# Root mean squares of four norms by token on partitions, and six modulation chunks summed off TensorE

## The reference

```python
def rms_norm(x, gain=None):
    y = x * lax.rsqrt(jnp.mean(x * x, axis=-1, keepdims=True) + 1e-6)
    return y if gain is None else y * gain

cond = jax.nn.silu(c)
for layer in range(2):
    mod = cond @ ada_w[layer] + ada_b[layer]            # (1024) @ (1024 x 6144)
    sh_m, sc_m, g_m, sh_f, sc_f, g_f = jnp.split(mod, 6, axis=-1)
    h = rms_norm(x) * (1 + sc_m) + sh_m
    mix = dsa_mixer(h, ...) if layer == 0 else gated_deltanet_mixer(h, ...)
    x = x + g_m * mix
    h = rms_norm(x) * (1 + sc_f) + sh_f
    x = x + g_f * peer_ffn(h, ...)
return rms_norm(x, final_norm)
```

## Time and profile before

| | |
|---|---|
| time, median of 3 runs (lowest, highest) | 3556.41 us (3554.92, 3565.26) |
| the profiled execution's own time | 3563.29 us |
| its span, first to last instruction | 3561.3 us |
| mean granted TensorE clock | 0.991 |
| busy share: PE, DVE, ACT, POOL | 97%, 73%, 50%, 32% |
| attention (with norm0 and modulations), about | 0 to 340 us |
| norm1, norm2, norm3, norm4, about | 340 to 360, 1642 to 1663, 2254 to 2276, 3541 to 3561 us |

### The profile page before, as it was taken

How to read it: one execution, slowest core, us unless ns; L and a number is a source line. 1 busy time by engine, 2 the same in 40 slices (tenths; PEclk the granted TensorE clock), 3 DMA queues, 4 the chain that set the end, 5 groups by cost and what they waited for, 6 DMA issues and landing times.

```text
span 3561.3 us, 62918 instructions
## 1 busy us (share of the span) xinstructions
PE 3445.7 (97%) x20018; PEld 3155.0 (89%) x20018; DVE 2604.0 (73%) x4767; ACT 1777.1 (50%) x3224; POOL 1144.1 (32%) x866
## 2 busy tenths in 40 slices
PE   7999999999999999998999999899999999999998
PEld 4556899999999999996777697699999999999997
DVE  2755767579996888886888543576669996888887
ACT  3364345567773333335775233345557875333333
POOL 2102342534441222223664002343444442222222
PEclk9999999999999999999999999999999999999998
DMA  7564345789999999993556652235698999999995
GB/s 243 178 190 154 99 150 175 270 313 352 374 377 373 341 344 337 338 340 103 162 168 187 176 150 76 81 120 171 196 348 300 378 375 371 367 349 348 343 350 198
DMA packets 519872, 914.11 MB, mean 257 GB/s; under 512 B 70352, under 2 KB 359248, under 8 KB 511312
## 3 DMA queue, kind: packets, MB, share of 16 engines
q1 hardware_dynamic: 446032, 644.23, 52.9%
q0 software_dynamic: 73728, 268.47, 21.2%
HBM read 782.54 MB, written 130.02 MB: 256 GB/s over the span
## 4 chain that ended last, share of the span: by engine, by line
PE 81%; DVE 6%; ACT 5%; issue 3%; DMA 3%; SPq 1%; POOL 1%; DVEq 0%; ACTq 0%; POOLq 0%
PE bank L783 10%; PE bank L785 10%; PE bank L784 10%; PE bank L855 10%; PE bank L856 10%; PE bank L857 10%; PE bank L831 4%; PE bank L1010 2%; DVE oh L2592 2%; PE bank L479 2%; DVE rows L2563 1%; PE bank L1019 1%; DMA w_ring<-b_w_in 1%; PE bank L572 1%; PE bank L794 1%
## 5 line engine op out<-in xcount | busy, mean ns | idle before, releaser
L783 PE MATMUL bank<-hx,hl 128*128 128x384 f32 (+1 forms) x2304 | 798.6, 347 | 0.7 <-POOL hl L1579 0.7
L784 PE MATMUL bank<-hx,hl 128*128 128x384 f32 (+1 forms) x2304 | 786.2, 341 | 0.0
L785 PE MATMUL bank<-hx,hl 128*128 128x384 f32 (+1 forms) x2304 | 786.1, 341 | 0.0
L855 PE MATMUL bank<-W,hl 128*128 128x384 f32 x2016 | 679.8, 337 | 7.4 <-DVE W L2630 7.4
L856 PE MATMUL bank<-W,hl 128*128 128x384 f32 x2016 | 679.5, 337 | 0.0
L857 PE MATMUL bank<-W,hl 128*128 128x384 f32 x2016 | 679.5, 337 | 0.0
L1602 POOL DMA_INDIRECT rows<-p_v,erow x256 | 262.4, 1025 | 858.4 <-DVE xtok L2637 836.4
L1602 POOL DMA_INDIRECT rows<-p_u,erow x256 | 358.9, 1402 | 406.3 <-DVE rows L2563 368.0
L1910 ACT ACTIVATE hl<-hT 128x1024 fp32r<-128x1024 f32 x272 | 287.6, 1057 | 362.5 <-PE bank L857 317.4
L1910 ACT ACTIVATE hl<-w_ring 128x1024 fp32r<-128x1024 f32 x272 | 287.4, 1057 | 344.6 <-PE bank L857 311.7
L783 PEld LDWEIGHTS bank<-hx,hl 128*128 128x128 f32 x2304 | 434.6, 189 | 10.9 <-POOL hl L1579 0.9
(11 more groups left out here) (372 smaller groups left out, 5507.0 us busy)
## 6 DMA issues: line engine op xcount, KB each, us to landing
w_ring<-p_u_t SPq DMA_DIRECT2D x128, 512.0 KB
hT<-p_u_t SPq DMA_DIRECT2D x128, 512.0 KB
w_ring<-p_v SPq DMA_DIRECT2D x128, 512.0 KB
hT<-p_v SPq DMA_DIRECT2D x128, 512.0 KB
act_scratch<-hT SPq DMA_DIRECT2D x256, 192.0 KB
g_scratch<-gst SPq DMA_DIRECT2D x48, 1024.0 KB
gg<-g_scratch SPq DMA_DIRECT2D x64, 768.0 KB
ua<-act_scratch SPq DMA_DIRECT2D x256, 192.0 KB
```

The costliest lines, as they stand in the source:

```text
L783: nc.tensor.matmul(bank[s][:, c:], hi, hx[:, 0, k, c:], start=(k == 0), stop=False)
L784: nc.tensor.matmul(bank[s][:, c:], hi, hx[:, 1, k, c:], start=False, stop=False)
L785: mm = nc.tensor.matmul(bank[s][:, c:], lo, hx[:, 0, k, c:], start=False, stop=(k == KD - 1))
L855: nc.tensor.matmul(bank[j][:, P:], hi, W[:, s, 0, :], start=first, stop=False)
```

## The change

It does these things:

1. Chunks 4 to 9 of the modulations leave TensorE's row product. Chunks 4 to 7 are multiplied by the condition and summed over k on VectorE (`ada_product`, 8 instructions a chunk, in front of the scoring). Chunks 8 and 9 are multiplied in place by ScalarE (`ada_scaled`, at m = 3 and 4) and added up on GpSimd in three instructions (`ada_sums`). TensorE keeps the column products of all (`summed_columns`), at other places, and into bank 4. Chunks 10 and 11 keep their row products, behind tiles m = 6 and 7.
2. The low parts of weight tiles 2 to 7 move from GpSimd to VectorE (`in_low` in the VectorE part), between the products of item 1.
3. `INDEXED`: the last two pairs of the indexer move from tile m = 2 to m = 3, and the keys' tiles come one tile later with that.
4. The 16 rounds over tt = 1 move into the scoring of tt = 2 and 3: one "8 largest" and one strike-out for each of the 16 scores. The loop behind is over tt = 2 and 3 alone.
5. The bias of chunks 4 to 11 is added at head step 2, no longer in front of `maxima(0)`. The `+ 1` of the scales is made from the bank in one instruction.
6. Norms 1 to 4: the sums come out with tokens on partitions, as 4 columns of bank 2, by 8 products with one column of ones; root and inverse are on 128 x 4 elements; 4 products of the inverse, spread over 128 weight columns, with the identity spread it to 128 x 512 in bank 2, which VectorE then reads as its second operand instead of `rstd`. VectorE frees bank 2 behind the last of the eight multiplications.
7. The queue of transfers: chunk 6 is loaded before tile 6, chunks 7 to 9 behind tiles 7 to 9, chunks 10 and 11 behind tile 14. A chunk's slot is free when its predecessor is summed.

```diff
@@ constants
-           [(3, 0), (3, 1), (3, 2), (3, 3)]]
+           [(3, 0), (3, 1)], [(3, 2), (3, 3)]]
+ADA_FIRST, ADA_LAST = 4, 12
+ADA_BY_DVE = 8
+ADA_SCALED_AT = {8: 3, 9: 4}
+ADA_ROWS_AT = {10: 6, 11: 7}
+ADA_COLUMNS_AT = {4: -1, 5: -1, 6: 0, 7: 0, 8: 6, 9: 7}
+LOW_BY_POOL = 8
@@ TensorE, norm_added
                 take(2)
-                pe.wait_ge(sem("squares_added"), (KD - 2) * times)
-                nc.tensor.matmul(bank[2][:, :], ones[:, :], hT[:, 0, :], start=True, stop=False)
-                pe.wait_ge(sem("squares"), t.turn("squares", KD) + KD)
-                nc.tensor.matmul(bank[2][:, :], ones[:, :], hT[:, KD - 1, :], start=False, stop=True
-                                 ).then_inc(psum_full[2], 1)
+                squares = t.turn("squares", KD) + KD
+                order = (0, KD - 1) if times % 2 else (KD - 1, 0)
+                for k in order:
+                    if k == 0:
+                        pe.wait_ge(sem("squares_added"), (KD - 2) * times)
+                    else:
+                        pe.wait_ge(sem("squares"), squares)
+                    for tt in range(TT):
+                        mm = nc.tensor.matmul(bank[2][:, tt:tt + 1], hT[:, k, tt * P:(tt + 1) * P], ones[:, 0:1],
+                                              start=(k == order[0] and tt == 0), stop=(k == order[1] and tt == TT - 1))
+                mm.then_inc(psum_full[2], 1)
+
+                take(2)
+                pe.wait_ge(sem("columns_ready"), 1 + times)
+                for tt in range(TT):
+                    mm = nc.tensor.matmul(bank[2][:, tt * P:(tt + 1) * P], rstd[:, tt:tt + 1].to_broadcast([P, P]), ident[:, :],
+                                          start=True, stop=True)
+                mm.then_inc(psum_full[2], 1)
@@ TensorE, attention
-                take(3)
-                for m in range(KD):
-                    in_tile(7 + m, m % 2, between=(lambda k, m=m: indexed(m, k)) if m < len(INDEXED) else None)
-                    ada_rows(4 + m)
-                    if m > 0:
-                        ada_columns(3 + m)
+                take(4)
+                for m in range(-1, KD):
+                    if m >= 0:
+                        in_tile(7 + m, m % 2, between=(lambda k, m=m: indexed(m, k)) if m < len(INDEXED) else None)
+                    for n in ADA_ROWS_AT:
+                        if ADA_ROWS_AT[n] == m:
+                            ada_rows(n)
+                    for n in ADA_COLUMNS_AT:
+                        if ADA_COLUMNS_AT[n] == m:
+                            summed_columns(n).then_inc(sem("ada_turned"), 1)
...
-                ada_columns(11).then_inc(psum_full[3], 1)
+                summed_columns(10)
+                summed_columns(11).then_inc(psum_full[4], 1)
@@ SyncE
                 for m in range(4):
                     load_in(3 + m, C_QI + m * P)
+                    if m == 2:
+                        load_ada(6)
...
-                for m in range(2):
+                for m in range(KD):
                     load_in(7 + m, m * P)
-                for m in range(KD):
-                    if m + 2 < KD:
-                        load_in(9 + m, (m + 2) * P)
-                    if 6 + m < 12:
-                        load_ada(6 + m)
+                    if m < 3:
+                        load_ada(7 + m)
+                for n in range(10, ADA_LAST):
+                    load_ada(n)
@@ GpSimd
-            for i in range(2, 15):
+            def ada_sums(n):
+
+                part = ada_slot(n)
+                pool.wait_ge(sem("ada_scaled"), KD * (n - ADA_BY_DVE + 1))
+                pool.wait_ge(sem("ada_turned"), n - ADA_FIRST - 1)
+                for step, width in enumerate((4, 2, 1)):
+                    to = part[:, 0:width, :] if width > 1 else ada_sum(n).unsqueeze(1)
+                    if step > 0:
+                        pool.wait_ge(sem("ada_summed"), ada_summed(n - 1) + step)
+                    nc.gpsimd.tensor_tensor(to, part[:, 0:width, :], part[:, width:2 * width, :], ALU.add
+                                            ).then_inc(sem("ada_summed"), 1)
+
+            for i in range(LOW_BY_POOL, 13):
                 in_low(i)
+            ada_sums(8)
+            in_low(13)
+            ada_sums(9)
+            in_low(14)
@@ ScalarE, norm
-                nc.scalar.activation(rstd[:, :], bank[2][:, :], ACT.Sqrt, scale=1.0 / D, bias=eps[:, 0:1]
+                n = T if stage == "norm0" else TT
+                nc.scalar.activation(rstd[:, 0:n], bank[2][:, 0:n], ACT.Sqrt, scale=1.0 / D, bias=eps[:, 0:1]
                                      ).then_inc(psum_free[2], 1)
@@ VectorE
-                ins.then_inc(sem("mods_ready"), 1)
...
+                step(nc.vector.tensor_tensor(flat[:, first:last], bank[b][:, first:last], added[:, first:last], ALU.add))
                 for c in scales:
-                    ins = nc.vector.tensor_scalar(flat[:, c:c + KD], flat[:, c:c + KD], 1.0, None, ALU.add)
+                    ins = nc.vector.scalar_tensor_tensor(flat[:, c:c + KD], bank[b][:, c:c + KD], 1.0, added[:, c:c + KD],
+                                                         ALU.add, ALU.add)
...
-                step(nc.vector.reciprocal(rstd[:, :], rstd[:, :]))
+                if nth == 0:
+                    step(nc.vector.reciprocal(rstd[:, :], rstd[:, :]))
+                else:
+                    nc.vector.reciprocal(rstd[:, 0:TT], rstd[:, 0:TT]).then_inc(sem("columns_ready"), 1)
+                    full(2)
+                inverse = rstd[:, :] if nth == 0 else bank[2][:, :]
...
+                if nth > 0:
+                    dve.wait_ge(sem("hn_ready"), KD * (nth + 1))
+                    dve.sem_inc(psum_free[2], 1)
...
+                def ada_product(n, first, last):
+
+                    to = ada_sum(n)
+                    for k in range(first, last):
+                        if k == 0:
+                            dve.wait_ge(sem(f"ada_loaded{n % 2}"), 16 * (n // 2))
+                            ins = nc.vector.tensor_scalar(to, ada_slot(n)[:, k, :], cond[:, k, 0:1], None, ALU.mult)
+                        else:
+                            dve.wait_ge(sem("ada_summed"), KD * (n - ADA_FIRST) + k)
+                            ins = nc.vector.scalar_tensor_tensor(to, ada_slot(n)[:, k, :], cond[:, k, 0:1], to, ALU.mult, ALU.add)
+                        ins.then_inc(sem("ada_summed"), 1)
```

More of the change, by code:

```diff
@@ L228, in hybrid_trunk @@
         probT = sb("probT", [P, 2, 2, TT, T], where=part)
+        mx = sb("mx", [P, 8], where=part)
+        nmx = sb("nmx", [P, 8], where=part)
+        rowsum = sb("rowsum", [P, 8], where=part)
+        rinv = sb("rinv", [P, 8], where=part)
         stage_ = ExitStack()
@@ L521, in ada_columns, with summed_columns @@
                 return mm
+            def summed_columns(n):
+                if n in ADA_ROWS_AT:
+                    pe.wait_ge(psum_free[ada_bank(n)], marks[f"ada{n}"])
+                    part = ada_part[:, n % 2, :]
+                else:
+                    pe.wait_ge(sem("ada_summed"), ada_summed(n))
+                    part = ada_sum(n)
+                for c in range(4):
+                    mm = nc.tensor.matmul(bank[4][:, 4 * n + c:4 * n + c + 1], part[:, c * P:(c + 1) * P],
+                                          ones[:, 0:1], start=True, stop=True)
+                return mm
@@ L2319, in attention, with largest, taken, masked @@
                 ins.then_inc(sem("ckv_ready"), 1)
+                ada_product(5, KD // 2, KD)
+                in_low(5)
+                ada_product(6, 0, KD)
+                in_low(6)
+                ada_product(7, 0, KD // 2)
+                in_low(7)
+                ada_product(7, KD // 2, KD)
+                def largest(tt):
+                    return nc.vector.max(top8[:, tt, :], score[:, tt, 0:(tt + 1) * P])
+                def taken(tt):
+                    return nc.vector.match_replace(score[:, tt, 0:(tt + 1) * P], top8[:, tt, :],
+                                                   score[:, tt, 0:(tt + 1) * P], TAKEN)
+                def masked(tt):
+                    return nc.vector.memset(score[0:CHUNK, tt, tt * P + CHUNK:(tt + 1) * P], NEG)
                 for n in range(TT * IH):
@@ L2324, in attention @@
                     b = 5 + n % 3
+                    if n == 2 * IH:
+                        step(masked(1))
+                    if n >= 2 * IH:
+                        largest(1).then_inc(sem("dve_step"), 1)
                     dve.wait_ge(psum_free[b], t.turn(b) + 1)
                     if n == 0:
-                        dve.wait_ge(sem("idx_ready"), 6)
+                        dve.wait_ge(sem("mixer_ready"), 7)
                     w = widx[:, tt, h:h + 1]
@@ L2334, in attention @@
                     ins.then_inc(sem("relu_used"), 1)
+                    if n >= 2 * IH:
+                        dve.wait_ge(sem("dve_step"), t.turn("dve_step") + 1)
+                        step(taken(1))
```

(18 more changed lines are left out.)

99 lines of the change are left out of this document (63 added, 36 removed).

## The result

| | before | changed |
|---|---|---|
| time, median | 3556.4 us (20 runs, 3551.1 to 3569.4) | 3536.3 us (20 runs, 3528.7 to 3559.5) |
| changed / before, with 95% interval | | 0.9949 (0.9938 to 0.9959) |
| profiled execution, own time (span) | 3563.3 (3561.3) | 3547.2 (3545.4) |
| mean granted TensorE clock | 0.991 | 0.990 |

The account below looks back on a forecast made before the run. TensorE was taken as the bound (81% of the chain), in attention by only some 4 us over VectorE. Gains less losses in attention and the norms summed to 22.5 us, so 3556.4 becomes 3533.9 us, range 3524 to 3547.

Parts of the forecast that it names:

- attention: Stage before norm1: row products 11.1, first score 1.3, first modulations 1.3 gained, less 1.5 us of new waits.
- norm1: Norm before the first peer stage: 2.0 us lost around the fourth late chunk's wait for bank 2, bounds +0.2 and -3.5.
- norm2: From GpSimd's last sum to the first multiplication: shorter root, inverse and spreading gain 3.8 us as the middle.
- norm3: Norm before the second peer stage, without late chunks: block 0 ready earlier, 4.7 us gained.
- norm4: Last norm: shorter root, inverse and spreading gain 3.8 us, near the slow end of its span.
- Row products: Attention: six chunks' row products leave TensorE, 1.85 us each, gaining 11.1 us if what replaces them is covered.
- The first modulations: Start: the `+ 1` reads a bank, takes 0.2 instead of 1.61 us, and 1.3 us of it is kept.
- The first score: Attention: two column sets ahead shrink the clash with GpSimd's low part to some 0.4 us, gaining 1.3.
- New waits: Attention: low parts and chunk loads arriving within about 1 us cost TensorE 1.5 us, between 0 and 8.
- The column products stay eight sets: nothing: Attention: TensorE keeps as many column products, 0.94 us a set, so they change the time by nothing.
- The interleaved selection: Scoring to heads: VectorE's masks come about 4 us late, covered up to 8.25 us by the third head pair's bank; price 0.
- The first rival: Norms: GpSimd still holds VectorE's multiplications despite the bank input; gain 11.2 us, time 3545, chance 0.12.

## Why the prediction was right

The forecast was 3534, in a range of 3524 to 3547; it is 3536.3. The sum was 22.5 us; the stages, over all traces, give 17.0, and the time 18 by the ratio (15 to 22). That the median came within 3 us of the forecast, though the sum was some 5 too large, is in part luck. The mechanisms held, and most sizes were somewhat large:

| term | predicted | measured |
|---|---|---|
| attention (11.1 + 1.3 + 1.3 - 1.5) | 12.2 | 12.4 at the heads in the two profiles; 11.6 at norm1's last square (341.0 in 2 traces, 329.4 in 5) |
| norm1 | -2.0 | -3.5 (20.9 in 2 traces, 24.4 in 7) |
| norm2 | 3.8 | 2.6 (8.5 in 2 traces, 5.9 in 11) |
| norm3 | 4.7 | 3.3 |
| norm4 | 3.8 | 3.0 (8.4 in 2 traces, 5.4 in 11) |

- *Row products, 11.1, with what replaces them covered*: right. TensorE waits twice in the stage, 0.42 and 0.41 us, no more than before.
- *The first modulations, +1.3*: the `+ 1` does take 0.17 in all. The first product of the weight tiles starts at 43.8 in the two traces without the change and at 42.3 in the five with it, 1.5 earlier; how much of that is the `+ 1` is open, since this start moves by 2.2 between the five.
- *The first score, +1.3*: a draw. TensorE waits for it between 0 and 2.0 us in the eleven traces with item 2, 1.07 in the middle one, against 1.35 before: GpSimd's low part meets VectorE's last product or the score, by where ScalarE stands.
- *New waits, 1.5*: there were none, but 1.7 us lost at half clock behind the 16 column records at m = 0 and again behind the 24 before the heads. "The column products stay eight sets: nothing" is the part that failed. It counted records, not what they do to the clock.
- *The interleaved selection, price 0*: right, but "covered up to 8.25 us" was not. The room is 4. I looked for the third head pair's bank and passed over the values' bank, which ScalarE empties in its own order. Had the masks come 4 us late, as I reckoned, there would have been nothing in hand; they came 1.3 late.
- *Norm1*: the fourth chunk stood alone, behind 5.73 us, not 4.2, and at half clock: at the low bound of -3.5, in three of seven traces beyond it (-3.9 to -4.2). The chunk starts 14.0 to 14.1 us behind the last square in all seven, 12.4 was reckoned; in the changed kernel's profile 1.3 of this is the held first low part ahead of five of the multiplications, which the term left out.
- *Norm3, 4.7*: I applied the case of two SBUF inputs to the multiplications and not to the low part 2 us behind, which GpSimd now holds for 1.2 us. The earlier trace rows could not show it: there the low part came after GpSimd was done.
- *Norms 2 and 4*: the time between the last square and the first block depends on GpSimd's sums and the clock at that moment (7.9 and 9.1 before, 5.5 to 7.1 after, for norm2), and the earlier trace rows is of one execution, a slow one for both.

The first rival (GpSimd holds the multiplications too) is out: 673 to 687 ns for all 32. The Trainium skill (SBUF — State Buffer, "SBUF: two separate sides") says that only a VectorE operation in its two-port mode, or with two SBUF inputs while GpSimd reads SBUF, excludes GpSimd's. The rows on two inputs agree: 1.88 against 4.91 us. The one-input `+ 1` of the earlier trace rows could be a case of the two-port mode, but no row names an instruction's mode.

## What to carry to other kernels

When a shorter step frees the path, look at what its buffer was shared with: a bank that is now held for eight multiplications instead of one root cost norm1 all that it had gained, and another bank gave it back. With GpSimd at work, put one of VectorE's two inputs in PSUM, and check every instruction from SBUF to SBUF that the earlier start moves under GpSimd, those with one input too. A wait costs more than its length when the clock falls behind it. And scatter one-column products: behind 24 or 32 in a row the clock fell in 8 of 8 traces.

## What I had not expected of the hardware

**Two rates at one granted clock.** In the dense products of a peer stage TensorE does either 568 or 579 products in 100 us, both at clock 1.00 and without a gap. Windows of the kernel before, and of the changed one:

```profile
1272.00:1372.00 100.00, 100.00 (x568) 100.00 (x567) 81.27 (x95) 35.33 (x48) 23.88 (x24) 1.00 0.95 339
3270.00:3370.00 100.00, 100.00 (x579) 100.00 (x578) 82.94 (x97) 35.53 (x49) 24.41 (x25) 1.00 0.97 347
```

```profile
1272.00:1372.00 100.00, 100.00 (x579) 100.00 (x578) 82.90 (x97) 35.36 (x48) 24.22 (x24) 1.00 0.97 347
3270.00:3370.00 100.00, 100.00 (x568) 100.00 (x567) 81.14 (x95) 34.98 (x48) 23.21 (x23) 1.00 0.95 338
```

It goes by stage and execution, not by kernel: of 14 traces three have the slow rate in `peer(0)` and two in `peer(1)`, never both, and each costs some 11 us (the rest of `peer(1)` takes 1264.8 to 1268.4 us at the fast rate, 1276.1 and 1277.3 at the slow one). That is the +10.2 and -11.4 of the first table, and would be a large part of the spread of the times, which no run shows apart: for a stage of some 20 us one trace tells more than twelve times do. What sets the rate stays open.

**The clock falls while TensorE is busy.** With TensorE busy throughout, the granted clock was 0.50 for 3.4 us behind 16 one-column records in a row at tile m = 0 and behind 24 before the heads (7 of 7 traces each), and for 6.8 us from within the 32. The count alone does not decide: behind 16 in a row elsewhere in attention it fell in 2 of 14 cases (1 of 7 ahead of tile m = 0; before the heads 1 of 4 with the sets apart, 0 of 2 with the attention of before, 0 of 1 in the kernel with 32). At tile m = 0 another 16 had gone before, some 12 us earlier; whether that matters is open.
